# Expert weights of a mixture-of-experts layer: two transfers of 512 KB in place of one of 1 MB

## What is computed

```python
def body(acc, blk):
    tok, w, e = blk                       # 128 slots of one expert
    xb = x_pad[tok]
    h = jax.nn.silu(xb @ w_gate[e]) * (xb @ w_up[e])
    return acc.at[tok].add((h @ w_down[e]) * w[:, None]), None
```

## Time and profile before

| | before |
|---|---|
| median of 3 runs | 3209.09 us (3208.25 to 3211.19) |
| the profiled execution's own time | 3206.43 us |
| its span (first to last instruction) | 3204.6 us |
| PE, PEld, DVE, ACT, POOL busy | 85%, 60%, 55%, 44%, 34% of the span |
| granted TensorE clock, mean | 0.934 of full |
| DMA | 696.98 MB in 158408 packets, mean 217 GB/s |
| largest queue, q1 | 113648 packets, 607.41 MB |

### The profile page before, as it was taken

One profiled execution on the slowest core, in us unless ns is written; L12 is line 12 of the kernel. 1 busy time (PEld: TensorE's weight loads), 2 busy tenths in 40 slices (PEclk: granted clock), 3 DMA queues, 4 the chain that ended last, 5 costly groups with the idle time before them and its releaser, 6 DMA issues. The chain is left out here.

```text
span 3204.6 us, 37715 instructions
## 1 busy us (share of the span) xinstructions
PE 2735.3 (85%) x12402; PEld 1938.2 (60%) x12402; DVE 1772.5 (55%) x2185; ACT 1416.6 (44%) x1946; POOL 1076.3 (34%) x763
## 2 busy tenths in 40 slices
PE   7979999897699999999970488885769999999990
PEld 2346677674466676666750477774646777666660
DVE  7823244534556655566638465565266555556546
ACT  5521233421156666666641232332115666666650
POOL 1000000022445555555535300000244555555543
PEclk9989999998899999999995799997889999999995
DMA  9930100013179999999967101102228999999976
GB/s 357 325 115 14 40 1 1 25 58 145 35 284 377 387 384 367 379 379 380 362 227 327 61 20 40 40 1 76 107 79 310 379 361 342 352 356 346 346 264 249
DMA packets 158408, 696.98 MB, mean 217 GB/s; under 512 B 33976, under 2 KB 45240, under 8 KB 100464
## 3 DMA queue, kind: packets, MB, share of 16 engines
q1 hardware_dynamic: 113648, 607.41, 50.1%
q0 software_dynamic: 43520, 84.21, 7.0%
q10 hardware_dynamic: 1152, 4.19, 0.4%
HBM read 680.91 MB, written 86.08 MB: 239 GB/s over the span
## 5 line engine op out<-in xcount | busy, mean ns | idle before, releaser
L1570 DVE TENSOR_TENSOR F_gu_lo<-gu_raw,F_gu_hi 128x2048 fp32r<-128x2048 f32 x292 | 661.4, 2290 | 592.0 <-ACT F_gu_hi L1515 583.2
L1515 ACT ACTIVATE F_gu_hi<-gu_raw 128x2048 fp32r<-128x2048 f32 x292 | 553.6, 1917 | 75.2 <-DMA gu_raw<-in_we_up_dram 51.0
L1464 PE MATMUL F_psY<-d_raw,F_hT 128*128 128x512 f32 x1168 | 525.6, 593 | 2.9 <-ACT F_hT L1533 2.9
L102 PE MATMUL F_psG<-F_gu_hi,F_xT_hi 128*128 128x512 f32 x1168 | 470.7, 403 | 7.5 <-DVE F_xT_lo L1562 7.5
L104 PE MATMUL F_psG<-F_gu_hi,F_xT_lo 128*128 128x512 f32 x1168 | 458.5, 393 | 0.0
L103 PE MATMUL F_psG<-F_gu_lo,F_xT_hi 128*128 128x512 f32 x1168 | 457.1, 391 | 0.0
L1391 POOL DMA_INDIRECT F_xb<-f_d,F_gi x146 | 321.9, 2205 | 129.5 <-POOL F_gi L1388 122.5
L1464 PEld LDWEIGHTS F_psY<-d_raw,F_hT 128*128 128x128 f32 x1168 | 211.2, 191 | 212.9 <-issue 209.5
L1529 ACT ACTIVATE F_yb<-F_psY,wgt 128x1024 f32<-128x1024 f32 x146 | 163.0, 1117 | 362.0 <-PE F_psY L1464 362.0
L1388 POOL COPY F_gi<-gat 128x1 int32 (+1 forms) x146 | 303.7, 2080 | 23.7 <-PE F_psX L1447 23.6
L102 PEld LDWEIGHTS F_psG<-F_gu_hi,F_xT_hi 128*128 128x128 f32 x1168 | 222.0, 190 | 50.9 <-DVE F_xT_lo L1562 9.8
(11 more groups left out here) (311 smaller groups left out, 4413.2 us busy)
## 6 DMA issues: line engine op xcount, KB each, us to landing
gu_raw<-in_we_gate_dram SPq DMA_DIRECT2D x146, 1024.0 KB, 8.9
gu_raw<-in_we_up_dram SPq DMA_DIRECT2D x146, 1024.0 KB
d_raw<-in_we_down_dram SPq DMA_DIRECT2D x146, 1024.0 KB, 7.0
wada<-in_w_ada_dram SPq DMA_DIRECT2D x24, 2048.0 KB
H_y<-y_d SPq DMA_DIRECT2D x10, 4096.0 KB
I_w_raw<-in_wc_in_dram SPq DMA_DIRECT2D x32, 384.0 KB, 5.5
f_d<-D_f SPq DMA_DIRECT2D x10, 512.0 KB, 2.6
fT<-in_wa_out_dram SPq DMA_DIRECT2D x6, 512.0 KB, 6.4
```

Source lines behind the costliest of these rows:

```text
L102: nc.tensor.matmul(acc, xh, wh, start=(start and i == 0), stop=False)
L1464: ins = nc.tensor.matmul(psY[:, n], hT[:, j, k], d_raw[:, j, k, c], start=(k == 0), stop=(k == KF - 1))
L1515: nc.scalar.activation(gu_hi[:, j, v], gu_raw[:, j, v], ACT.Copy).then_inc(s_guh, 1)
L1570: V.tensor_tensor(gu_lo[:, j, v], gu_raw[:, j, v], gu_hi[:, j, v].bitcast(F32), ALU.subtract).then_inc(s_gul, 1)
```

## The change

`load_weights` issues two transfers along the second axis, the two halves of each partition's 8192 bytes, so a packet carries 4096 bytes. Both halves add 16 to the same semaphore, so every wait on `s_raw` counts to twice its value. Nothing else is changed: no buffer, no wait of SP, no order of blocks.

```diff
                 dst, src = moe.d_raw[:, j], a["we_down"][l, bass.ds(e, 1)].rearrange("o (p k) n -> p (o k) n", p=P)
-            eng.dma_start(dst, src).then_inc(moe.s_raw[j][m], 16)
+            n = dst.shape[1] // 2
+            for k in (slice(0, n), slice(n, 2 * n)):
+                eng.dma_start(dst[:, k], src[:, k]).then_inc(moe.s_raw[j][m], 16)
...
-                                down_of(i - 1, 1 - j, 16 * q)
+                                down_of(i - 1, 1 - j, 32 * q)
...
-                        split_gate_up(0, 16)
+                        split_gate_up(0, 32)
...
-                                split_gate_up(1 - j, 16 * q + 16)
+                                split_gate_up(1 - j, 32 * q + 32)
```

More of the change, by code:

```diff
@@ L1494, in _ @@
                                 turn_rows(1 - j)
-                                down_of(i - 1, 1 - j, 16 * q)
+                                down_of(i - 1, 1 - j, 32 * q)
                         i = 2 * m + 3
                         front(i, 1)
-                        down_of(i - 1, 0, 16 * m + 32)
+                        down_of(i - 1, 0, 32 * m + 64)
                         pe.wait_ge(s_mul, i + 1)
                         turn_hidden()
-                        down_of(i, 1, 16 * m + 32)
+                        down_of(i, 1, 32 * m + 64)
                     @block.scalar
@@ L1515, in split_gate_up @@
                                 nc.scalar.activation(gu_hi[:, j, v], gu_raw[:, j, v], ACT.Copy).then_inc(s_guh, 1)
-                        split_gate_up(0, 16)
+                        split_gate_up(0, 32)
                         act.wait_ge(s_tx, 1)
                         rows()
-                        split_gate_up(1, 16)
+                        split_gate_up(1, 32)
                         act.wait_ge(s_gu, 1)
```

## The result

The changed kernel takes 3236.68 us, median of 5 runs (3231.86 to 3242.38), beside 3209.09 before: a ratio of 1.0091 with a 95% interval of 1.0076 to 1.0106. It is slower by 27.6 us (29 by the ratio), where 3198 was forecast and 3226 was the end of the range. The profiled execution spans 3234.9 us.

The account below looks back on a forecast made before the run. PE (10.0 us a block) and DMA were taken as both nearly full, with PE the floor, lengthened by late gathers. From 3206.43 us profiled, 29.4 won and 18 lost gave 3195.0, or 3198 on the median; range 3180 to 3226, own bounds 3188 to 3202.

Parts of the forecast that it names:

- term 2: Weight queue q1: three matrices in shorter packets cost 0.23 us more a block, delaying landings without bounding by itself.
- the sum of terms: Whole kernel: 29.4 us won and 18 us lost, 3198 us on the median, bounds 3188 and 3202; chance 0.43.
- third rival: Expert stages: weights become the bound through ACT's up wait, DVE's low part and PE's L102; 3222 us, chance 0.27.
- Term 1: PE's waits for gathered rows: gathers beside shorter weight packets land 1.2 us sooner, winning 29.4 of 30.4 us.
- Term 3: Up matrix loses queue share to gathers, lands about 0.5 us later, and through ACT and DVE costs PE 18 us.
- Terms at nothing: SP's three extra issues a block, 1.2 us, covered by its waits; later up issue covered by queue backlog; no cost.
- mild form: Late weights in the expert stages: 40 us lost against 29 won, 3220 us, taken as 3222.
- dear form: DMA engines: 0.03 us belonging to each packet adds 0.7 us a block, 100 us in all, with nothing won.
- The rule of large transfers: Weight DMA: at least 1 MiB a transfer for full bandwidth; serial fixed cost would add 6 us a block, some 880 us.
- The other sentence of those rules: Weight DMA: splitting a transfer into two halves is not worth it, as they share the same engines.

Follow-up runs that it names:

- one_of_4096: Kernel before, still one 1 MB transfer a matrix, but a 64-byte gap in SBUF between row halves makes packets 4096 bytes: 3221.33 us beside 3204.36, ratio 1.0054.
- experiment 8, halves_contiguous: Changed kernel, with each half read as one contiguous 512 KB piece of HBM and PE's transposes reordered to match: 3204.02 us beside 3206.02, ratio 0.9997.
- experiment 1: Kernel before, one 1 MB transfer a matrix, packets cut to 4096 bytes by a 64-byte SBUF gap: 3221.33 us beside 3204.36, ratio 1.0054.
- experiment 6: Against the change, matrices cut by interleaved partitions: even/odd with 8192-byte packets 3190.44 us, even/odd with 4096-byte packets 3199.58, four transfers of every fourth partition 3219.78.
- odd_even_4096: Against the change, two transfers a matrix cut by even and odd partitions, with 4096-byte packets by a 64-byte SBUF gap: 3199.58 us, ratio 0.9982 to before.
- experiment 5: SP issues gate and up ahead of the down matrix it issued first: 3269.97 us with the kernel before's transfers, 3224.12 us with the change's halves.
- experiment 4, gather_first: Kernel before, with POOL issuing each gather a block earlier, packets still 8192 bytes: 3203.98 us, ratio 0.9993.
- two_by_odd_even: Against the change, two 512 KB transfers a matrix cut by even and odd partitions, packets of 8192 bytes: 3190.44 us, ratio 0.9945 to before.
- experiment 2: Against the change, two transfers a matrix cut by partitions 0 to 63 and 64 to 127, packets of 8192 bytes: 4017.39 us, ratio 1.2535 to before.

## Why the prediction was wrong

**The step that failed is term 2**, "It does not bound by itself", and with it the sum of terms as if each could be paid alone. one_of_4096 is what the three terms describe, short packets and nothing else new. Its added work is close to the forecast: 8.43 us of q1 a block where before has 8.16, 0.27 more beside 0.23, and 2.81 us a MiB beside 2.73, the 0.08 of the earlier trace rows. Yet it lost 17 us, where the terms sum to 11 us won. So the addition was sized right and still it cost time. The work before was taken as 9.8 us a block, a mean over a longer window; from 1000 to 1600 it is 9.98, and 0.27 more passes the point which the third rival had named: "once the engines' work passes 10.0 us a block". The second stage shows that this point is no sharp one: one_of_4096 has 9.84 us of queues a block there and still takes 10.35 us where before takes 10.22.

What the prediction did not have at all is the rest of the change's 0.44 us: in its halves a MiB costs 2.88 us and not 2.81, by the pitch at which they are read (experiment 8).

By the ratios the parts of the change are, against before: short packets +17 us in one transfer (experiment 1) and +12 in two (experiment 6); two interleaved transfers in place of one -18 us with long packets and -23 with short ones; reading at a pitch of 8192, +30 us. The prediction had the effect of the first with the wrong sign, took the second for nothing, and did not have the third. That they nearly add up (17 - 23 + 30 = 24, by the ratio 29) is no test of them: the 5 us are just the distance between odd_even_4096 and halves_contiguous, at which one part ends and the next begins.

**Term 1** was right in its mechanism: the gathers' waits fell from 30.4 to 2.2 us, and the pair of experiment 5 shows it at work. Its 29.4 us were not to be had, since the same wait could be removed in the kernel before for no gain (experiment 4).

**Term 3** named the right chain, from ACT's up matrix by DVE's low part to L102, and far too small a size: 18 us forecast, where waits of PE's weight loads for DVE rose by some 77 us, part of which replace the gathers' (PE's idle time in the two windows rose by 19.4 us). It moved only the up matrix, and only in the 71 blocks where ACT waited already; gate is late as well, 81.3 us of ACT's waits, and a late gate moves both low parts. The expected L102 wait was 10 to 25 us; it is 45.4. Nor do the bounds of the sum follow from this term: with the 40 us that it allows the upper one is 3220 us, not 3202.

**Terms at nothing**: SP's issues cost nothing, as forecast. SP still waits 387.1 us in 69 blocks:

```profile
SPq L1367 <- PE F_psY L1466: 387.1, 69, 7.2
```

And two_by_odd_even issues as many transfers and is faster.

**The rivals.** The third happened, by its place and by its point, at 3237 us and not 3222, a net loss of 28 us: between its mild form (13) and its dear one (100). The sign that the prediction named for it came, a mean block above 10.2 us with DVE's wait in it: 10.57 and 10.41 us in the windows of the earlier trace rows. Its argument for the dear form, that a packet has a price of its own inside the stage, is not borne out: short packets take 0.27 us more a block and not 0.7. The rule of large transfers in the Trainium skill ("DMA: Bandwidth & Descriptors", Rules for kernel authors) had pointed to slower, but two_by_odd_even speaks against its reason here: twice the transfers, 512 KB each, 0.55% faster. The other sentence of those rules that the prediction drew on speaks of disjoint partition halves, and the change's halves are none. Its reason, that both share the same engines, holds for experiment 2 and two_by_odd_even alike, and the one takes 4017 us and the other 3190.

## What to carry to other kernels

Where PE and the DMA queues both stand near 95%, don't count a wait on the path as won before it is removed by an edit of its own: here it moved to another buffer (gather_first). The queues' time a block beside PE's tells that this can happen, not by how much. Test a loss by cutting bytes; if it goes with them, it hangs on the queues' load. If a transfer must be cut, give every part partitions from the whole range, keep its packets long and its reads in HBM in one piece, and only then look for who waits.

## What was not expected of the hardware

- Transfers into 64 neighbouring partitions: 239 GB/s where 377 is usual, with engines 100% busy. That neighbouring partitions are the cause is inferred from this against two_by_odd_even (380 GB/s); the path behind them was not measured. One transfer of 128 KB into 16 neighbours cost 1.2 us a block, but it also read the same bytes each time.
- Reading 4096 bytes at a pitch of 8192 in HBM: 2.88 us a MiB against 2.81 in one piece. Reading 8192 bytes at a pitch of 16384 (two_by_odd_even) shows no such price: 2.71, beside 2.73 for one transfer.
- Two interleaved transfers are faster than one, and four slower than two. Why is open, as is the reason for the price of the pitch: nothing was run that looks inside the memory.
